# 32 tokens moved from the dense first product of a PEER layer to gathered rows and dot products

## The reference

```python
qry = (xb @ w_q).reshape(TB, PEER_HEADS, PEER_D_KEY)      # 8 heads
s1, s2 = qry[..., :half] @ keys_1.T, qry[..., half:] @ keys_2.T
# top 16 of each, top 16 of their 256 sums -> 16 experts of 16384 per head and token
idx = i1 * 128 + i2
gate = softmax(sc)
act = gelu(einsum('thed,td->the', u_table[idx], xb))
y = einsum('the,thed->td', gate * act, v_table[idx])
```

## Time and profile before

| | value |
|---|---|
| time of the profiled execution | 1564.76 us |
| its span | 1563.0 us |
| median of three other runs | 1565.91 us |
| PE busy | 1515.3 us (97%) |
| DVE busy | 1223.1 us (78%) |
| ACT busy | 561.5 us (36%) |
| POOL busy | 547.2 us (35%) |
| mean granted TensorE clock | 0.989 of full speed |
| DMA, mean over the span | 256 GB/s |
| PE in the chain that ended last | 83% |

### The profile page before, as it was taken

How to read it: one execution, slowest core, us unless ns; L and a number is a source line. 1 busy time by engine, 2 the same in 40 slices (tenths; PEclk the granted TensorE clock), 3 DMA queues, 4 the chain that set the end, 5 groups by cost and what they waited for, 6 DMA issues and landing times.

```text
span 1563.0 us, 22972 instructions
## 1 busy us (share of the span) xinstructions
PE 1515.3 (97%) x8069; PEld 1353.2 (87%) x8069; DVE 1223.1 (78%) x2336; ACT 561.5 (36%) x816; POOL 547.2 (35%) x297
## 2 busy tenths in 40 slices
PE   6999989999989999999999999979999999999999
PEld 6879658788989999999999999968888888888887
DVE  4537473288989999989999999648878788787886
ACT  4363442222423333334444444333232332322321
POOL 2213241232643222752333323314434434344341
PEclk9999979999999999999999999999999999999999
DMA  5400202221467877997798898999999999999993
GB/s 198 142 28 1 108 1 67 87 75 68 162 226 266 276 260 258 367 413 289 296 324 311 284 332 309 356 327 373 354 350 355 352 356 354 351 359 349 354 355 125
DMA packets 181667, 399.37 MB, mean 256 GB/s; under 512 B 12260, under 2 KB 111844, under 8 KB 180072
## 3 DMA queue, kind: packets, MB, share of 16 engines
q1 hardware_dynamic: 144744, 264.41, 48.3%
q0 software_dynamic: 36864, 134.23, 23.3%
HBM read 346.16 MB, written 52.43 MB: 255 GB/s over the span
## 4 chain that ended last, share of the span: by engine, by line
PE 83%; DVE 8%; POOL 3%; DMA 3%; issue 1%; ACT 1%; SPq 0%; DVEq 0%; ACTq 0%
PE banks L1820 25%; PE banks L1613 15%; PE banks L1884 11%; PE banks L1886 11%; PE banks L1885 11%; PE banks L1855 5%; POOL u_rows L669 3%; DMA u_rows<-in_u,idx 1%; DMA v_raw<-in_v 1%; PE banks L1801 1%; PE banks L1664 1%; DVE wo_lo L1241 1%; PE banks L1723 1%; DVE picked L1385 1%; PE banks L1748 1%
## 5 line engine op out<-in xcount | busy, mean ns | idle before, releaser
L669 POOL DMA_INDIRECT u_rows<-in_u,idx x128 | 202.9, 1585 | 362.8 <-DVE z L1423 336.7
L691 POOL DMA_INDIRECT v_rows<-in_v,idx x128 | 205.5, 1606 | 333.4 <-DVE x_res L1550 294.8
L1884 PE MATMUL banks<-v_hi,w_hi 128*128 128x512 f32 x768 | 299.6, 390 | 7.4 <-DVE v_lo L1497 7.4
L1886 PE MATMUL banks<-v_hi,w_lo 128*128 128x512 f32 x768 | 299.3, 390 | 0.0
L1885 PE MATMUL banks<-v_lo,w_hi 128*128 128x512 f32 x768 | 299.3, 390 | 0.0
L1497 DVE TENSOR_TENSOR v_lo<-v_raw,v_hi 128x1024 fp32r<-128x1024 f32 x128 | 153.6, 1221 | 120.4 <-ACT v_hi L982 120.4
L982 ACT ACTIVATE v_hi<-v_raw 128x1024 fp32r<-128x1024 f32 x128 | 125.8, 1049 | 339.0 <-PE banks L1886 320.2
L1820 PE MATMUL banks<-h_lo,u_hi 128*128 128x384 f32 x1024 | 209.9, 338 | 0.0
L1820 PE MATMUL banks<-h_hi,u_lo 128*128 128x384 f32 x1024 | 199.2, 335 | 9.5 <-DVE u_lo L1412 9.5
L1820 PE MATMUL banks<-h_hi,u_hi 128*128 128x384 f32 x1024 | 203.6, 340 | 0.3 <-ACT u_hi L909 0.3
L1820 PEld LDWEIGHTS banks<-h_hi,u_lo 128*128 128x128 f32 x1024 | 179.4, 188 | 11.1 <-DVE u_lo L1412 11.1
(11 more groups left out here) (256 smaller groups left out, 1926.2 us busy)
## 6 DMA issues: line engine op xcount, KB each, us to landing
u_raw<-in_uT SPq DMA_DIRECT2D x128, 512.0 KB
v_raw<-in_v SPq DMA_DIRECT2D x128, 512.0 KB, 5.9
act_scratch<-act_out SPq DMA_DIRECT2D x128, 192.0 KB
act_in<-act_scratch SPq DMA_DIRECT2D x32, 768.0 KB, 8.4
gates<-gate_scratch SPq DMA_DIRECT2D x32, 768.0 KB, 12.4
gate_scratch<-stage SPq DMA_DIRECT2D x11, 2048.0 KB, 8.1
wi_raw<-in_w_in SPq DMA_DIRECT2D x8, 1024.0 KB, 8.7
wq_raw<-in_w_q SPq DMA_DIRECT2D x8, 1024.0 KB, 5.6
```

What stands on the lines that cost most here:

```text
L669: nc.gpsimd.indirect_dma_start(u_rows[U_SLOT[s]][:], None, a["u"], bass.IndirectOffsetOnAxis(ap=idx0[:, s:s + 1], axis=0)).then_inc(ug_in[ ...
L691: nc.gpsimd.indirect_dma_start(v_rows[s % V_ROWS][:], None, v_flat, bass.IndirectOffsetOnAxis(ap=idx0[:, s:s + 1], axis=0)).then_inc(vg_in ...
L1884: mm(y, w, v_hi[q][:, j, ds], start=first and j == 0, stop=False)
L1886: end = mm(y, w_lo[q][:, j, t * P:(t + 1) * P], v_hi[q][:, j, ds], start=False, stop=last and j == GROUP - 1)
```

## The change

The first token block beyond the sparse one gives 32 tokens (128 to 159) to the sparse way for u only: the first product goes over 352 columns; the activations of the 32 tokens are computed by 32 further gathers and dots, on all 128 partitions as 4 groups of 32 tokens with a quarter of the slots each (`idx1`, `h2x`, `z1`). Their Gelu result is multiplied into their gates (`tab[:, 0, 0:32]`), and the second product, which still goes over 384 tokens, sees 1.0 as their activation. The batches of gates are rotated so that these tokens come last. From expert block 16 to 118 POOL makes u_lo of every even block, when DVE opens it with a small memset, right ahead of two dots. h2 of token block 0 is copied into PSUM banks 2 and 3 (its SBUF place holds `h2x` then), so z has 2 banks. Every second one-hot tensor is made by ACT: four Squares of iota minus token value and one Relu of one minus that. Dots stand by a table: two in each even step from 14, one of the new ones in 32 steps from 47 to 103, three and one in turn from 104.

```diff
-T0 = P
+NE = 32
+NA = ND - NE
+T1 = P + NE
-POOL_SPLITS = 12
+POOL_FIRST, SHARE_FROM = 12, 16
+Z_BANKS = 2
+SHARED = list(range(SHARE_FROM, POST, 2))
+DOTS = [""] * POST + ["aa"] * 4 + [""] * 4
+for _n in range(POST):
+    if _n + 2 in SHARED:
+        DOTS[_n] = "aa"
+for _n in [*range(PRE - 25, PRE, 2), *range(PRE + 1, PRE + 32, 2), PRE + 4, PRE + 14, PRE + 24]:
+    DOTS[_n] += "b"
+for _n in range(PRE + 32, POST):
+    DOTS[_n] += "a"
-DOT_SIZE, SLOT_SIZE = 1170, 2800
+PIECE_SIZE = 2150
...
             for h in range(PH):
...
+                if h == 1:
+                    sp.wait_ge(h2_ready, 2)
+                    sp.dma_start(h2x_d, h2_nat[0:NE, H2_SLOT[1], :]).then_inc(h2x_saved, 16)
...
-                sp.dma_start(act_in[q][:], act_d[bass.ds(g * GROUP, GROUP)].rearrange("n p t -> p n t")
+                sp.dma_start(act_in[q][:, :, NE:], act_d[bass.ds(g * GROUP, GROUP)].rearrange("n p t -> p n t")
...
+                kind, x = ORDER[s]
+                if kind == "b" and x == 0:
+                    pool.wait_ge(idx1_ready, 1)
+                    for y in range(P // NE):
+                        nc.gpsimd.dma_start(idx1[y * NE:(y + 1) * NE, :], idx1n[0:NE, y * NE:(y + 1) * NE]
+                                            ).then_inc(idx1_in, 16)
+                    pool.wait_ge(idx1_in, 16 * (P // NE))
...
+            for n in range(len(DOTS)):
+                while s < len(ORDER) and (U_BEFORE[s] is None or U_BEFORE[s] < len("".join(DOTS[:n]))):
+                    gather_u(s)
+                    s += 1
+                if n + 2 in SHARED:
+                    pool.wait_ge(share_open, SHARED.index(n + 2) + 1)
+                    split_u(n + 2)
...
+            for j in (2, 3):
+                emptied(act, JOBS[(len(JOBS) - 1) // 8 * 8 + j][0])
+            nc.scalar.activation(h2_first, h2_nat[:, 0, :], ACT.Copy).then_inc(h2_placed, 1)
...
+            def one_hot(i, b):
+                slot, m = b % OH_RING, i * (MAIN_BATCHES // 2) + (b // 2)
+                for w in range(BATCH):
+                    at_t = tab[:, 2, bass.ds(token(i, b, w), 1)]
+                    nc.scalar.activation(oh2[:, slot, w, :], iota, ACT.Square, bias=at_t, scale=-1.0
+                                         ).then_inc(oh_square, 1)
+                act.wait_ge(oh_square, m * BATCH + BATCH)
+                nc.scalar.activation(oh2[:, slot, :, :], oh2[:, slot, :, :], ACT.Relu, bias=1.0, scale=-1.0
+                                     ).then_inc(oh_scalar, 1)
...
                     take_gates(i, 2 * j, first)
+                    if not (last and j == MAIN_BODY - 1):
+                        one_hot(i, 2 * j + 3)
...
-                nc.vector.tensor_tensor_reduce(rows[:], rows[:], h2_nat[:, 0, :], 1.0, 0.0, ALU.mult, ALU.add,
-                                               z0[:, n:n + 1]).then_inc(dot_done, 1)
+                h2, z = (h2_first, z0) if kind == "a" else (h2x[:], z1)
+                nc.vector.tensor_tensor_reduce(rows[:], rows[:], h2, 1.0, 0.0, ALU.mult, ALU.add,
+                                               z[:, x:x + 1]).then_inc(dot_done, 1)
...
+            def splits_and_dots(n):
+                if n + 2 in SHARED:
+                    nc.vector.memset(opened[:, SHARED.index(n + 2):SHARED.index(n + 2) + 1], 0.0).then_inc(share_open, 1)
+                else:
+                    split_u(n + 2)
+                for _ in DOTS[n]:
                     dot()
...
+                    if PRE + i * MAIN_BODY + j == SCALE_AT:
+                        dve.wait_ge(z1_ready, 1)
+                        step(nc.vector.transpose(z1t[:], z1[:]))
+                        settle()
+                        step(nc.vector.tensor_tensor(tab[:, 0, 0:NE], tab[:, 0, 0:NE], z1t[:], ALU.mult))
+                        settle()
...
-            dve.wait_ge(dot_done, SLOTS)
+            dve.wait_ge(dot_done, len(ORDER))
+            dve.wait_ge(z_done, POST)
+            step(nc.vector.memset(act_in[0][:, :, 0:NE], 1.0))
+            dve.wait_ge(gate_saved[1], 16 * CHUNKS // 2)
+            step(nc.vector.memset(act_in[1][:, :, 0:NE], 1.0))
+            settle()
             weights(0, 0, True)
...
-                    pe.wait_ge(act_ready, n - (RING - 1))
-                o, q = ps[:, j % RING, 0:ND], j % ring
+                    pe.wait_ge(act_ready, n - (Z_BANKS - 1))
+                o, q = ps[:, j % Z_BANKS, 0:NA], j % ring
...
-                    last = mm(o, u[:, q, k, :], h2[:, k, T0:], start=m == 0, stop=m == PER_BLOCK - 1)
+                    last = mm(o, u[:, q, k, :], h2[:, k, T1:], start=m == 0, stop=m == PER_BLOCK - 1)
```

More of the change, by code:

```diff
@@ L281, in build @@
         tab = at("tab", 186, [P, 3, ND])
+        opened = at("opened", 103.25, [P, len(SHARED)])
+        h2x = at("h2x", 182, [P, D])
+        idx1n = at("idx1n", 103.5, [P, SLOTS], I32)
+        idx1 = at("idx1", 19.875, [P, NE], I32)
+        z1 = at("z1", 19.625, [P, NE])
+        z1t = at("z1t", 103.125, [P, NE])
         idx0 = at("idx0", 20, [P, SLOTS], I32)
@@ L969, in main @@
                     take_gates(i, 2 * j + 1, first)
+                    if isinstance(i, int) and i == GELU_TRIP and j == 2:
+                        act.wait_ge(dot_done, len("".join(DOTS[:PRE + GELU_TRIP * MAIN_BODY])))
+                        nc.scalar.activation(z1[:], z1[:], ACT.Gelu).then_inc(z1_ready, 1)
             main(0, True)
-            with act.Fori(1, MAIN_TRIPS - 1) as i:
+            with act.Fori(1, GELU_TRIP) as i:
                 main(i)
+            main(GELU_TRIP)
             main(MAIN_TRIPS - 1, last=True)
@@ L1439, in _ @@
                 pass
-            def rest():
-                for t in range(1, TB):
-                    made = choose(t)
-                    for size in CHOOSE_SIZES:
-                        if next(made, 0) is None:
-                            yield size
-                        if size > 1500 and dots[0] < DOTS_PRE:
-                            dot()
-                            yield DOT_SIZE
-                while dots[0] < DOTS_PRE:
-                    dot()
-                    yield DOT_SIZE
-            work, done = rest(), 0
-            for n in range(POOL_SPLITS - 2, PRE):
-                split_u(n + 2)
-                while done < (n - POOL_SPLITS + 3) * SLOT_SIZE:
-                    done += next(work, SLOT_SIZE)
+            def splits_and_dots(n):
+                if n + 2 in SHARED:
+                    nc.vector.memset(opened[:, SHARED.index(n + 2):SHARED.index(n + 2) + 1], 0.0).then_inc(share_open, 1)
+                else:
+                    split_u(n + 2)
+                for _ in DOTS[n]:
+                    dot()
+            work, done = itertools.chain(*(choose(t) for t in range(1, TB))), 0
+            sizes = itertools.cycle(CHOOSE_SIZES)
+            for n in range(POOL_FIRST - 2, PRE):
+                splits_and_dots(n)
+                while done < (n - POOL_FIRST + 3) * PIECE_SIZE:
+                    done += next(sizes)
+                    next(work, None)
                 if n == NORM_AT:
@@ L1465, in _ @@
                                                    ps[:, 4 + t, 0:3 * P].rearrange("p (w t) -> p w t", w=3)))
-            for _ in work:
-                pass
+            assert next(work, 0) == 0
             settle()
+            dve.sem_inc(tab_ready, 1)
             def one_hots(n):
@@ L1490, in _ @@
                             one_hots(i * MAIN_BATCHES + 2 * j + 2 + n)
-                    for _ in range(DOTS_MAIN[j]):
-                        dot()
             def split_v(g, q, j):
@@ L1516, in post_dots @@
             def post_dots(n):
-                for _ in range(DOTS_POST[n - POST]):
+                for _ in DOTS[n]:
                     dot()
@@ L1860, in main @@
                     between = [((b + 1) * PER_BATCH - 1 - j * PER_BLOCK,
-                                lambda b=b: gate_matrices(i * MAIN_BATCHES + b, b, first and b < 4))
+                                lambda b=b: gate_matrices(i, b, first and b < 4))
                                for b in BATCHES_IN[j]]
-                    first_product(i * MAIN_BODY + (PRE + j), j, between=between)
+                    first_product(i * MAIN_BODY + (PRE + j), j, i, PRE + j, MAIN_BODY, between=between)
             main(0, True)
```

139 lines of the change are left out of this document (94 added, 45 removed).

## The result

The changed kernel takes 1543.73 us, the median of four runs (1542.02 to 1549.56), beside 1565.6 us before. The ratio is 0.9865, 95% interval 0.9845 to 0.9886: faster by 1.35%, 21.9 us. Six more runs beside eleven of before gave 0.9870 (0.9846 to 0.9893). The profiled execution was the slowest of the first four, 1549.56 us with a span of 1547.5, so its rows account for 15.5 us of span and not for 22. The second profile of the same kernel (in the table as "again") has a span of 1539.1.

The account below looks back on a forecast made before the run. PE was taken to set the end, with VectorE a hair behind and pacing the stretch ahead of main. 9.2 + 11.4 - 0.6 = 20 us off the profiled 1564.8 gives 1544.8, as a median 1546 us; range 1525 to 1563.

Parts of the forecast that it names:

- Step 1: First product: 352 columns take 160.2 ns a matmul, a block 3.84 us, 0.32 less; the first twelve blocks give nothing.
- Steps 2 and 3: Ahead of main: VectorE sets the pace, GpSimd's splits cost 10 us; main begins at 693.8, 9.2 us earlier.
- The argument on PSUM: Beside GpSimd's splits: dots reading h2 from PSUM do not contend, so two dots (2.3 us) can run through a split.
- step 3: Ahead of main: split tails delay pieces, and GpSimd late behind gathers stalls VectorE up to 1.4 us; 10 us in all.
- Step 4: Main: PE needs 5.63 us a block and VectorE keeps up; main 11.4 us shorter, ending at 968.6.
- The ring: Main from step 104: four row buffers refill late, 11 us of slip, mostly hidden; 4 us charged (0 to 11).
- Step 5: Behind main: first weights wait for the tail of the gates, delaying block 125's split; 0.6 us lost.
- The wait that I had named: Behind main: first weights wait until the gates' tail is stored, 24.8 us after block 120 began; PE waits 2 us more.
- (a): Rival, ahead of main and in it: GpSimd always in time, row buffers hold; gain 34 us, 1532 us; 25%.
- (b): Rival, from block 56 on: DMA is the bound at 355 GB/s, 20 us more, 1566 us; 12%.
- (c): Rival, ahead of main and in it: dots collide with GpSimd's splits, 2.4 us each; 73 us more, 1619 us; 6%.
- (d): Rival, main: ScalarE reloads tables twice a block, 7.3 us instead of 5.63; 1619 us; 5%.

Follow-up runs that it names:

- run on widths alone: No layer computed: groups of 48 matmuls, one width each, on an otherwise idle chip; all groups of 352 columns but the first took 7.95 to 8.01 us.
- the last wait for gate rows moved: Changed kernel with VectorE waiting for the last save of gates only ahead of the second group's weights; 1543.36 us, ratio 0.9859.
- the whole stretch reordered: Changed kernel with VectorE's last gate wait later, Gelu before rounding u, last gate save behind block 126's u, v loads earlier; 1532.68 us, ratio 0.9785.

## Why the prediction was right, step by step

The forecast was 1546 us, the median is 1543.73, inside the range. The sum of the profiled pair was put at 20 us and was 15.5; of the second profile it is 23.9. The terms are less exact than the total. Forecast were 9.2 up to main, 11.4 in main and 0.6 lost behind it; measured were 12.1, 8.2 and 4.8 lost, and in the second profile 13.8, 11.9 and 1.8 lost. Too little in the first term and too much in the others partly cancel, so that the median came within 2.3 us of the forecast is in part luck.

**Step 1, narrower matmuls.** Their worth as an average holds. The price of 160.2 ns was from a line between two widths, and no stretch of the kernel runs at it: it is 158.3 or 166.7 (160.0 was seen in the run on widths alone). In main that is 5.59 or 5.77 us a block for the predicted 5.63; in the first profile 39 blocks x 0.14 = 5.5 us were lost to it, which is more than the 3.2 us by which main fell short of the predicted 11.4. That blocks of 3.84 and 5.63 us would be seen was wrong. The first twelve blocks gave nothing, as said: block 12 still waits for DVE.

**Steps 2 and 3, ahead of main.** DVE does pace this stretch, and the gain was larger than forecast: main began at 690.85 us, 12.1 earlier instead of 9.2. Block 56 began at 627.11 instead of 635.39 in the trace of before, 8.3 earlier where 4.1 were forecast, and from there the 16 blocks took 63.7 us (61.8 in the second profile; forecast 62.3). The contention is real, and near what was charged. From 447 us to the end of the choices VectorE's 23 splits took 32.0 us for 28.0 undisturbed (1216 ns each), and the two kinds of big pieces, six of each, 4.04 and 3.69 us in the mean for the 3.48 of both in the trace of before: together 8.6 us, where 10 were charged. The splits behind them, up to main, add 5 us more, for which the forecast had nothing. One of the pieces beside a late split and its gathers:

```profile
608.14 5.59 DVE L1491 TENSOR_TENSOR picked<-picked,pay 128x3200 f32<-128x3200 f32 x1
```
```profile
600.44 4.02 POOL L731 DMA_INDIRECT u_rows<-in_u,idx  x1 [0.16 <-issue]
604.77 1.96 POOL L731 DMA_INDIRECT u_rows<-in_u,idx  x1 [0.30 <-issue]
607.03 0.94 POOL L731 DMA_INDIRECT u_rows<-in_u,idx  x1 [0.30 <-issue]
607.98 2.38 POOL L715 TENSOR_TENSOR u_lo<-u_raw,u_hi 128x1024 fp32r<-128x1024 f32 x1
```

DVE had opened this split at 605.87 us, and it began at 607.98, behind two more gathers: the mechanism of step 3, but larger. The dots beside it were over and not half over, and the piece took 2.1 us more than 3.48, where at most 1.4 was forecast. The last piece of the choices ended at 625.2 us, five before the 630.2 of the forecast (447.2 + 173 + 10). With 8.6 us of contention in it, the work of VectorE without contention was 169.4 us, and the 173 that I had counted were some 4 too many. Two of them are the memsets, which run inside the time of a dot (759.59 above). That term and the contention, each a little too large, are what was mis-sized. The argument on PSUM is shown by the dots from SBUF: the Trainium skill's rule (SBUF — State Buffer, who interferes with whom) and the trace agree, with 1213 ns against 1853 for a dot.

**Step 4, main.** That DVE would keep up held: the price of the one-hots was right, and DVE's four gate rows, splits and dots took what the earlier trace rows say. The ring does slip: DVE stood 26.0 us for gathered rows in main, before 1.4, more than the 11 that I had bounded it by, but nearly all of it in DVE's own slack; PE lost 2.1 us, against 4 charged. ACT's new work cost nothing, as said.

**Step 5, POST.** The wait that I had named did come, but it was not the whole mechanism, and the price was too small: 3.7 us lost in the first profile and 1.5 in the second, 0.6 forecast. The tail of the gates was seen by SyncE 27.1 us after block 120 began, not 24.8 and 1 more, and VectorE stood 2.46 us for it:

```profile
995.94 0.39 SPq L590 DMA_DIRECT2D act_in<-act_scratch  x1
```
```profile
996.01 0.17 DVE L1654 MEMSET act_in<- 128x128 f32 x1 [2.46 <-DMA gate_scratch<-stage]
996.21 1.76 DVE L1624 TENSOR_TENSOR w<-act_in,gates 128x1536 f32<-128x1536 f32 x1
997.88 1.22 DVE L1521 TENSOR_TENSOR u_lo<-u_raw,u_hi 128x1024 fp32r<-128x1024 f32 x1
```

What I missed is, first, the clock: a wait of 2.33 us left it at 1.00, one of 6.16 brought it to 0.50 and cost 2 us more. And, second, ScalarE's queue: its rounding of u for block 125 stood 4.76 us for a transfer, with the Gelu of block 123 behind it, and with two z banks PE can't begin block 125 before that Gelu (the 2.12 us). PE needs the rounded u for that block as well, and it was there only 0.4 us sooner than the Gelu, so most of this wait is the transfer's. The second profile has no such wait. The account: 5.1 us more of waits and 2.0 of the clock, less 8 x 0.36 = 2.9 for blocks at the faster pace, is 4.2 for the 3.7 seen. Taking away the wait that I had named gave no time that could be measured; taking away the Gelu's place behind the rounding and the late loads as well gave 11.5, most of it from a wait that before had too.

**The rivals.** (a), all covered, did not come about in the changed kernel, since PE still waited 6.9 us for POOL's u_lo. (b), the DMA bound at 355 GB/s, fell: a window of main moved 408 GB/s at a share of 1.00 with PE at 20.00 of 20. The Trainium skill's figure that was cited with it (SBUF — State Buffer, a bandwidth-pool intuition that's wrong), near 358 GB/s for one core, does not hold here as a ceiling. By 358 instead of 355 the sum of (b) would have been 3 us less, not 2. (c) fell by the dots of 1213 ns, and the run with h2 in SBUF shows that it would have come: 1608 us, where I had 1619. (d) fell: ScalarE loaded no table in main, beside 48 one-hots. The columns not shortening was excluded, and rightly.

## What to carry to other kernels

Before work is moved to a second engine, look at where its operands lie: one operand in PSUM let a GpSimd subtraction and a VectorE reduction run side by side, and with both in SBUF the reduction took half as long again. After a stage is shortened, read the queues in front of the next one in order: here the order of a few waits, DMA issues and Gelus was worth more than half of what the change itself gave. And a matmul width should be timed in place, over several executions, before it is given a price from a line.

## What was not expected of the hardware

First, the same 24 matmuls of 352 columns run at 158.3 or 166.7 ns each at the same granted clock, the pace being kept until a stall; with 384 columns only 173.3 was seen, and in the run on widths, whose groups read from column 0 and from one tile alone, 352 columns ran at 160.0 to 161.1. Executions of the changed kernel differ by up to 11 us, and the profiled one was 6 us from the median; how much of that is the pace is not shown. Second, waits of PE of 2.91 (main, second profile), 6.16 and 7.18 us were followed by matmuls at half the granted clock, and cost 1.7, 2.0 and 3 us beyond themselves. The Trainium skill (TensorE: Matmul & The Clock Gate, The HAM clock gate) tells of a clock that idleness takes back, and the trace agrees. But the length of a wait alone does not tell what it costs. PE waited 2.93 us for u_lo of block 54 in both profiles of the changed kernel; in the first the clock stayed at 1.00, in the second it fell to 0.50:

```profile
621.92 1.55 PE L1943 MATMUL banks<-h_hi,u_lo 128*128 128x352 f32 x8 [2.93 <-POOL u_lo L715]
```
```profile
620.62 2.03 PE L1943 MATMUL banks<-h_hi,u_lo 128*128 128x352 f32 x8 [2.93 <-POOL u_lo L715]
```

In other runs a wait of 2.23 us was followed by half the clock (the last wait for gate rows moved) and one of 2.73 us was not (the whole stretch reordered).

Third, an indirect gather takes 0.94 us to issue beside a dot that reads PSUM, and 4.02 beside a two-input comparison or product of 3200 columns, both inputs in SBUF, so that GpSimd's queue is late exactly where VectorE is full. Fourth, 408 GB/s were moved in 20 us of main without a wait of PE, and 417 ahead of it.
